# Even mixer of a four-layer model: values feature by feature, bias table and its products earlier, the first chunk's convolution taps on ScalarE and GpSimd

## The chip, the cores and the metric

The kernel runs on one core of a Trainium2 chip. The metric is the device time of one execution in microseconds (us), given as the median of several runs. The engines are called PE (TensorE, matrix products), DVE (VectorE), ACT (ScalarE), POOL (GpSimd) and SP (SyncE, which here issues DMAs). PE's clock has two levels, 1.2 and 2.4 GHz; the profile gives the granted clock of a stretch as a share of the higher one.

## The reference, cut to what matters

The model runs a row of blocks over 512 tokens of 1024 features. The change touches one mixer of them, attention beside a gated convolution, which runs once:

```python
def _attn_conv_mixer(h, w_in, sinks, conv_w, conv_b, ln_g, ln_b, w_out, rel_bias):
    u = h @ w_in
    ...
    q = u[..., :o1].reshape(bsz, seq, N_Q_HEADS, HEAD_DIM)      # 8 heads of 64
    k = u[..., o1:o2].reshape(bsz, seq, N_KV_HEADS, HEAD_DIM)   # 2 heads of 64
    v = u[..., o2:o3].reshape(bsz, seq, N_KV_HEADS, HEAD_DIM)
    attn = _swa_sink_attention(q, k, v, sinks, rel_bias)        # window 128, bias table by distance
    glu = u[..., o3:o4] * jax.nn.sigmoid(u[..., o4:])           # 512 channels
    ... _causal_depthwise_conv(glu, conv_w, conv_b) ...         # 31 taps a channel
    ... _layernorm over the 512 channels, silu; then [attn, conv] @ w_out
```

The input of the mixer is a normalized residual stream, and its output is added to it.

## The kernel before

**Layout and products.** Activations lie feature by feature: 128 partitions hold 128 features, and the free axis is the 512 tokens. Each product with weights is done in three passes of fp32r matmuls, high part by high part, low part by high part and high part by low part (lines 510, 511, 512). A job is one load of 128 x 2048 weights, `w_raw`. ACT rounds it to `w_hi` (`split_w`, line 1109), DVE takes the difference `w_lo` (line 1684), and then PE runs the job's two segments: each is one accumulation of 24 matmuls of 128x512 into one PSUM bank. `w_hi` and `w_lo` have two buffers, so ACT and DVE prepare the next job while PE works on this one.

**The even mixer's stages.** "ein" is six jobs, q = 0 to 5. Jobs 0 to 3 give the gated convolution's input: from each, DVE makes one chunk of 128 channels (two evictions, `hid` and `taps_in`, line 2230), ACT the sigmoid (line 1474), and DVE the product `glu` (line 2233). Jobs 4 and 5 give the queries `eq`. "einv" is one job whose first half gives the keys (`kz`) and whose second half the values (`vz`). Then follow eight attention units (two head groups of four tokens' blocks each), and "wout1", the output product.

**The convolution.** There are four chunks, c = 0 to 3, of 31 taps each. Chunk 3 has 21 of its taps on PE, as products with diagonal matrices (`taps`, line 960), `TAPS_EACH` of them in a unit. The last tap of chunks 0 to 2 is a seed that ACT writes to `cy` (line 1477). All 100 other taps are DVE instructions that read `cy`, add a shifted `glu` times a column of weights, and write `cy` (`conv_taps`, line 2217): eight after each "ein" job from q = 1 on, the others behind the key's evictions, between the four `eb_lo`, and in the units.

**The bias.** A small product of `onehot` and `relb` (line 884) makes a row of biases by distance. DVE adds the mask (`diag`), SP writes it to `diag_scratch` and reads it back as a table `ebias`. PE turns that table with four products by `flip` (line 907, "flips"), ACT and DVE keep a high and a low part of each (`eb_hi` line 1483, `eb_lo` line 2262). All four must be there before the first scores.

**The unit loop.** In each step u, PE has the scores of unit u (`qk`, lines 924 to 926), the transposes of unit u - 2 (`turn`, line 937) and the products with the values of unit u - 3 (`pv`, line 948). The scores go to DVE for maxima, to ACT for exponentials, to POOL for normalizing. Two units fill one bank with a pair of heads' output, which ACT and DVE split to `e_hi[r]`, `e_lo[r]` for r = 0 to 3 (`keep_o(r)`, line 2293); `pv` of the next pair waits until the bank has been read. At the steps `LN_AT = (6, 8)` PE sums over channels for the layer norm (`layer_sums`, line 974): `layer_sums(0)` gives the mean, which DVE subtracts, ACT squares, and `layer_sums(1)` the variance. Behind that come ACT's root (line 1535), DVE's reciprocal (line 2322) and four multiplications of `cy` (line 2326), ACT's four silu (line 1508) and `e_hi` (line 1541), DVE's four `e_lo` (line 2330), and "wout1".

**What sets the order.** Every engine's instruction stream is in the order in which the code writes it, and semaphores hold an instruction until its inputs are there. No scheduler moves anything. On PE, `pv(6, 0)` stands ahead of "wout1" and waits for `keep_o(2)`. On DVE, `keep_o(2)` is written into step u = 8, ahead of the four multiplications of `cy`.

Of the kernel before, what the change touches and what calls it, by code (L numbers as in the profile page):

```python
# [31 lines left out]
P = 128  # L32
T = 512
# [51 lines left out]
STAGES += [("up2", 22, 16, 2), ("down2", 16, 11, 1), ("ein", 6, 16, 2), ("einv", 1, 16, 5), ("wout1", 4, 16, 2),  # L85
# [20 lines left out]
for _name in PREPS:  # L106
    H_COUNT[_name] = _at
    if _name in GAIN:
# [4 lines left out]
             "ein": 12, "einv": 1, "rec": 4, "lgate": 0, "rec_b": 4, "ogate": 8}  # L113
# [37 lines left out]
CS_BANKS = (2, 3, 4, 7)  # L151
Q_BANKS = (0, 1, 6)
# [3 lines left out]
TAPS_AT, TAPS_EACH, LN_AT = 0, 5, (6, 8)  # L156
UNITS = 2 * NH
LAM_STEPS = 18
# [37 lines left out]
def build(nc, a, stop_after=None):  # L196
    with ExitStack() as ctx:
# [155 lines left out]
        kvc_done = sem("kvc_done")  # L353
# [21 lines left out]
        glu_sig, glu_done, y_seed, y_tap, y_made = (sem(n) for n in ("glu_sig", "glu_done", "y_seed", "y_tap", "y_made"))  # L375
        bias_hi, ident_kept, taps_made, zeroed = sem("bias_hi"), sem("ident_kept"), sem("taps_made"), sem("zeroed")
        k_kept, v_kept, sinks_neg = sem("k_kept"), sem("v_kept"), sem("sinks_neg")
# [129 lines left out]
        def _(pe):  # L507
# [370 lines left out]
            def even():  # L878
# [3 lines left out]

                pe.wait_ge(e_loaded, 16 * 5)
                pe.matmul(bank[MISC][0:8, 0:BLOCK_F + 1], relb[:], onehot[:], start=True, stop=True).then_inc(diag_mm, 1)

                j = J0["einv"]
                pe.wait_ge(w_lo_done, j + 1)
                pe.wait_ge(acc_free, FREE0["einv"] - 3)
                for k in range(ND):
                    mm = three(bank[0][:], *tile_of(j % 2, k), h_hi[:, k], h_lo[:, k], k == 0, k == ND - 1)  # L890
                mm.then_inc(seg_done, 1)
                for t in range(NT):
                    pe.wait_ge(acc_free, FREE0["einv"] + t - 2)
                    cols = slice(t * P, (t + 1) * P)
                    for k in range(ND):
                        wh, wl = tile_of(j % 2, ND + k)
                        mm = three(bank[(t + 1) % 4][:, 0:P], h_hi[:, k, cols], h_lo[:, k, cols], wh, wl, k == 0,
                                   k == ND - 1)
                    mm.then_inc(seg_done, 1)
                pe.wait_ge(diag_vec, 1)  # L900
                turn_rs(PREP_OF["mixe"] + 1)

                pe.wait_ge(diag_in, 16)
                for i in range(4):
                    if i >= 2:
                        pe.wait_ge(bias_kept, i - 1)
                    pe.matmul(bank[5 + i % 2][:], flip[:], ebias[:, 2 * i:2 * i + 2].rearrange("p h s -> p (h s)"),
                              start=True, stop=True).then_inc(flipped, 1)

                def qk(u, t):  # L910
# [4 lines left out]
                    if u == 0 and t == 0:  # L915
                        pe.wait_ge(bias_kept, 4)
                        pe.wait_ge(ident_kept, 1)
                        pe.wait_ge(k_kept, 2)
                        pe.wait_ge(v_kept, NT)
                        pe.wait_ge(zeroed, 2)  # L920
# [7 lines left out]
                def turn(u, x):  # L928
# [3 lines left out]
                    if u >= 1:  # L932
                        pe.wait_ge(kept_a, 2 * (u - 1) + x + 1)
                    for kb in (2 * x, 2 * x + 1):
                        for t in range(kb, min(kb + 2, NT)):
                            to, at = (kb % 2 * 2 + t - kb) * P, P if t == kb else 0
                            mm = pe.transpose(bank[4 + x][:, to:to + P], eprobs[u % 3][:, t, at:at + P], ident[:])
                    mm.then_inc(turned, 1)

                def pv(u, x):  # L940

                    r, half = u // 2, u % 2
                    if half == 0 and x == 0 and r:
                        pe.wait_ge(o_lo_done, ND + r)
# [7 lines left out]
                def taps(first, last):  # L952

                    for tap in range(first, min(last, PE_TAPS)):
                        if tap == 0:
# [3 lines left out]
                            pe.wait_ge(rs_col_done, 2)  # L959
# [18 lines left out]
                for u in range(E_UNITS + 3):  # L978
                    now, back, last = u < E_UNITS, 2 <= u < E_UNITS + 2, u >= 3
                    if now:  # L980
                        qk(u, 0)
                        qk(u, 1)
                    if back:
                        turn(u - 2, 0)
# [113 lines left out]
        def _(act):  # L1098
# [368 lines left out]
            def even():  # L1467
                for c in range(6):
# [6 lines left out]
                    if 1 <= c < 4:  # L1475
                        act.wait_ge(glu_done, c)
                        act.activation(cy[:, c - 1], glu[:, c - 1, TAPS - 1:], ACT.Identity, bias=col("cb_b", c - 1),
                                       scale=col("cb_w", (TAPS - 1) * CC + c - 1)).then_inc(y_seed, 1)
                act.activation(ident_r[:], ident[:], ACT.Copy).then_inc(ident_kept, 1)
                split_w(J0["wout1"])  # L1480
                for i in range(4):
                    act.wait_ge(flipped, i + 1)
                    act.activation(eb_hi[:, 2 * i:2 * i + 2].rearrange("p h s -> p (h s)"), bank[5 + i % 2][:], ACT.Copy,
                                   scale=1.0 / QK_SCALE).then_inc(bias_hi, 1)

# [191 lines left out]
        def _(dve):  # L1677
# [270 lines left out]
            def rope_end(r, out):  # L1948
# [12 lines left out]
                if r == 4:  # L1961
                    for half in range(2):
# [3 lines left out]
                        ins.then_inc(roped if half else kvc_done, 1)  # L1966
# [21 lines left out]
            def attention_inputs():  # L1988
# [9 lines left out]
                for q in range(4):  # L1998
                    for n in (2 * q, 2 * q + 1):
                        dve.wait_ge(seg_done, SEG0["kproj"] + n + 1)  # L2000
                        if n < 4:

                            for half in range(2):
                                src = slice(half * HD, (half + 1) * HD)
                                g = 2 * (n % 2) + half
                                dve.tensor_tensor(kvc[0:HD, n // 2, g * T:(g + 1) * T], bank[n % 4][src], rs[src], ALU.mult).then_inc(kvc_done, 1)
                                ins = dve.tensor_tensor(kvc[HD:P, n // 2, g * T:(g + 1) * T - 1], bank[n % 4][src, 1:T],
                                                        rs[src, 1:T], ALU.mult)
                                ins.then_inc(acc_free if half else kvc_done, 1)
# [190 lines left out]
            def even():  # L2200

                todo = [(0, tap) for tap in range(TAPS - 1)]
                todo += [(c, tap) for tap in range(TAPS - 1) for c in (1, 2)] + [(CC - 1, tap) for tap in range(PE_TAPS, TAPS)]
                place = {step: i for i, step in enumerate(todo)}
                tapped_now = 0

                def conv_taps(count, end=3 * (TAPS - 1)):
                    nonlocal tapped_now
                    count = min(count, end - tapped_now)
                    for c, tap in todo[tapped_now:tapped_now + count]:  # L2210
                        if (c, tap - 1) in place:
                            dve.wait_ge(y_tap, place[c, tap - 1] + 1)
                        else:
# [3 lines left out]
                        dve.scalar_tensor_tensor(out=cy[:, c], in0=glu[:, c, tap:tap + T], scalar=col("cb_w", tap * CC + c),  # L2217
                                                 in1=cy[:, c], op0=ALU.mult, op1=ALU.add).then_inc(y_tap, 1)
# [3 lines left out]
                for q in range(6):  # L2222
# [650 lines left out]
```

## Time and profile before

| | |
|---|---|
| median of 3 runs | 3060.1 us (3057.92 to 3061.3) |
| profiled execution, its own time | 3060.17 us |
| its span in the trace | 3058.4 us |
| PE busy | 2989.5 us, 98% |
| DVE, ACT, POOL busy | 52%, 39%, 17% |
| mean granted clock of PE | 0.991 |

The span runs from the first instruction of the trace to the last; 1.8 us of the execution's time lie outside it. The even mixer, with the start of its output product, covers 1592 to 1775 us of the span.

### The profile page before, as it was taken

The numbers are of one execution on the slowest core, as the hardware profiler recorded it, in microseconds if no ns is written. First come the engines' busy times: TensorE is split into PE (matmuls) and PEld (weight loads), VectorE is DVE, ScalarE is ACT, GpSimd is POOL, SyncE is SP. The second block draws the span as 40 slices with busy tenths as digits, with TensorE's granted clock in tenths as the row PEclk, the third lists the DMA queues.
The fourth block names the chain that finished last, engine by engine and source line by source line (L and its number), as shares of the span: only waits on it lengthen the run. The fifth ranks groups of instructions, "written<-read, shape, count | busy, mean of one in ns | idle before, by whom it ended". The sixth has DMA issues, their size and how long they took to land.

```text
span 3058.4 us, 37147 instructions
## 1 busy us (share of the span) xinstructions
PE 2989.5 (98%) x13546; PEld 2455.6 (80%) x13546; DVE 1594.9 (52%) x1838; ACT 1194.0 (39%) x1589; POOL 528.3 (17%) x516
## 2 busy tenths in 40 slices
PE   7999999999999999999999899999999999999998
PEld 6888877777888888788887688888888887788887
DVE  6665366687566535533338843333433337743332
ACT  5554243488455424322232442222322226532221
POOL 1111011255211112111110211111111104511110
PEclk9999999999999999999999999999999999999999
DMA  4222333200222223222232022222322232222222
GB/s 165 96 96 84 101 119 102 76 1 1 86 97 98 83 94 113 96 96 92 85 112 85 15 83 96 96 89 95 106 96 96 82 110 97 83 97 96 92 86 84
DMA packets 47931, 273.42 MB, mean 89 GB/s; under 512 B 6448, under 2 KB 8160, under 8 KB 25568
## 3 DMA queue, kind: packets, MB, share of 16 engines
q1 hardware_dynamic: 47840, 272.19, 25.7%
q8 instruction: 58, 0.95, 0.1%
q14 instruction: 33, 0.27, 0.0%
HBM read 269.28 MB, written 2.11 MB: 89 GB/s over the span
## 4 chain that ended last, share of the span: by engine, by line
PE 89%; DVE 6%; ACT 2%; issue 1%; POOL 1%; DMA 0%; DVEq 0%; ACTq 0%; SPq 0%; POOLq 0%
PE bank L510 28%; PE bank L512 28%; PE bank L511 28%; PE bank L822 1%; DVE w_lo L1684 1%; ACT probs L1394 1%; PE bank L960 1%; PE bank L728 0%; PE bank L806 0%; DVE rc L2395 0%; PE bank L839 0%; PE bank L838 0%; PE bank L926 0%; PE bank L807 0%; POOL r_lo L2674 0%
## 5 line engine op out<-in xcount | busy, mean ns | idle before, releaser
L510 PE MATMUL bank<-h_hi,w_hi 128*128 128x512 f32 x2448 | 961.7, 393 | 12.9 <-DVE w_lo L1684 7.8
L511 PE MATMUL bank<-h_lo,w_hi 128*128 128x512 f32 x2448 | 955.6, 390 | 0.0
L512 PE MATMUL bank<-h_hi,w_lo 128*128 128x512 f32 x2448 | 955.5, 390 | 0.0
L1684 DVE TENSOR_TENSOR w_lo<-w_raw,w_hi 128x2048 fp32r<-128x2048 f32 (+2 forms) x282 | 575.3, 2041 | 527.8 <-ACT w_hi L1109 527.1
L1109 ACT ACTIVATE w_hi<-w_raw 128x2048 fp32r<-128x2048 f32 (+2 forms) x282 | 474.9, 1684 | 328.3 <-PE bank L512 301.1
L510 PEld LDWEIGHTS bank<-h_hi,w_hi 128*128 128x128 f32 x2448 | 460.3, 188 | 117.0 <-DVE w_lo L1684 11.3
L512 PEld LDWEIGHTS bank<-h_hi,w_lo 128*128 128x128 f32 x2448 | 460.5, 188 | 97.3
L511 PEld LDWEIGHTS bank<-h_lo,w_hi 128*128 128x128 f32 x2448 | 460.5, 188 | 96.4 <-issue 1.9
L510 PE MATMUL bank<-act_hi,w_hi 128*128 128x512 f32 x1056 | 411.6, 390 | 4.4 <-DVE w_lo L1684 4.4
L511 PE MATMUL bank<-act_lo,w_hi 128*128 128x512 f32 x1056 | 411.3, 390 | 0.0
L512 PE MATMUL bank<-act_hi,w_lo 128*128 128x512 f32 x1056 | 411.3, 389 | 0.0
L2542 POOL TENSOR_TENSOR act_lo<-hid,act_hi 128x512 f32 (+1 forms) x132 | 171.8, 1301 | 1274.5 <-ACT act_hi L1202 847.3
L2517 POOL TENSOR_TENSOR sq_sum<-sq_sum,sq 128x512 f32<-128x512 f32 x87 | 123.5, 1420 | 824.3 <-ACT sq L1139 824.3
L510 PEld LDWEIGHTS bank<-act_hi,w_hi 128*128 128x128 f32 x1056 | 198.3, 188 | 46.3 <-DVE w_lo L1684 5.6
L1813 DVE TENSOR_TENSOR hid<-bank,rs 128x512 f32<-128x512 f32 x88 | 60.9, 692 | 331.6 <-PE bank L512 331.6
L512 PEld LDWEIGHTS bank<-act_hi,w_lo 128*128 128x128 f32 x1056 | 198.3, 188 | 41.3
L511 PEld LDWEIGHTS bank<-act_lo,w_hi 128*128 128x128 f32 x1056 | 198.3, 188 | 41.1
L1202 ACT ACTIVATE act_hi<-hid 128x512 f32 (+1 forms) x88 | 55.8, 634 | 410.8 <-DVE hid L1816 410.8
L1136 ACT ACTIVATE h_hi<-x,vec 128x512 fp32r<-128x512 f32 (+1 forms) x72 | 51.9, 723 | 366.2 <-DVE x L1701 366.2
L1701 DVE SCALAR_TENSOR_TENSOR x<-bank,x 128x512 f32 (+1 forms) x72 | 49.7, 691 | 254.1 <-PE bank L512 254.1
L1200 ACT ACTIVATE silu_g<-taps_in 128x512 f32<-128x512 f32 x88 | 55.7, 633 | 264.3 <-DVE taps_in L1810 264.3
L1786 DVE SCALAR_TENSOR_TENSOR bank<-taps_in,vec,bank 128x512 f32<-128x512 f32 x176 | 120.0, 750 | 1.8 <-ACT bank L1174 1.8
(373 smaller groups left out, 3207.3 us busy)
## 6 DMA issues: line engine op xcount, KB each, us to landing
w_raw<-in_w_up SPq DMA_DIRECT2D x132, 1024.0 KB, 4.9
w_raw<-in_w_down SPq DMA_DIRECT2D x96, 704.0 KB, 4.0
w_raw<-in_w_wout SPq DMA_DIRECT2D x12, 1024.0 KB, 4.9
w_raw<-in_w_ple SPq DMA_DIRECT2D x16, 640.0 KB, 3.9
w_raw<-in_w_ein SPq DMA_DIRECT2D x6, 1024.0 KB, 4.9
w_raw<-in_w_kproj SPq DMA_DIRECT2D x4, 1024.0 KB, 5.1
w_raw<-in_w_qproj SPq DMA_DIRECT2D x4, 1024.0 KB, 4.9
w_raw<-in_w_ogate SPq DMA_DIRECT2D x4, 1024.0 KB, 4.9
```

The lines of the kernel that those rows point to most:

```text
L510: pe.matmul(out, wh, mh, start=first, stop=False)
L511: pe.matmul(out, wh, ml, start=False, stop=False)
L512: return pe.matmul(out, wl, mh, start=False, stop=final)
L1109: act.activation(w_hi[j % 2][:, 0:n], w_raw[j % 2][:, 0:n], ACT.Copy).then_inc(w_hi_done, 1)
L1136: act.activation(h_hi[:, m], x[:, m], ACT.Copy, scale=col(GAIN[prep], m)).then_inc(h_hi_done, 1)
L1200: act.activation(silu_g[:], taps_in[:, u, PAD:], ACT.Silu).then_inc(silu_done, 1)
L1202: act.activation(act_hi[:, f], hid[:, u], ACT.Copy).then_inc(act_hi_done, 1)
L1684: dve.tensor_tensor(w_lo[j % 2][:, 0:n], w_raw[j % 2][:, 0:n], w_hi[j % 2][:, 0:n].bitcast(F32), ALU.subtract).then_inc(w_lo_done, 1)
L1786: dve.scalar_tensor_tensor(out=acc, in0=taps_in[:, g, PAD - back:PAD - back + T], scalar=col(f"conv{l}_{tap}", g * NF + f), in1=acc, op0=A ...
L1813: dve.tensor_tensor(hid[:, u], bank[2 * u + 1][:], rs[:], ALU.mult).then_inc(acc_free, 1)
L2517: pool.tensor_tensor(sq_sum[:], sq_sum[:], sq[:], ALU.add).then_inc(sq_added, 1)
L2542: pool.tensor_tensor(act_lo[:, f], hid[:, u], act_hi[:, f].bitcast(F32), ALU.subtract)\
```

## The change

**Values.** The value product becomes feature by feature like the keys: one segment of 24 matmuls of 128x512 into bank 4, where there were 96 matmuls of 128x128 with the tokens as the output's partitions. DVE scales it by the norm factor into `hid`, PE transposes it in four blocks (`turn_values`) between the first scores and the first taps, and ACT copies the result into `vz` with two instructions. DVE's eight small evictions and the transposes of the norm factor for them go.

**Bias.** The `onehot` product moves from behind q = 5 to behind q = 3, and DVE's `diag` to q = 4, so that the scratch's two DMAs are issued earlier. The four flips move between the key and the value product, into four banks of their own. On ACT the four `eb_hi` move ahead of `split_w` of "wout1".

**Taps.** Chunk 0's 30 taps leave DVE. ACT multiplies the shifted `glu` by the tap's column into `sq` or `silu_g` in turn, six such products in each "ein" step from c = 1 on (`first_products`), and POOL adds them to `cy` one after the other. Product t waits until the sum t - 2 is done, since it writes the tile that this sum read. Chunks 1 and 2 gather in PSUM banks 5 and 6, and move to `cy` in SBUF with the last tap before the units. DVE has 70 taps left, 31 in the "ein" steps, 6 behind the four `eb_lo`, 33 in the units. `TAPS_EACH` goes from 5 to 6, and `LN_AT` from (6, 8) to (5, 7). `keep_o(2)` is no longer pulled forward.

The settings and PE:

```diff
-TAPS_AT, TAPS_EACH, LN_AT = 0, 5, (6, 8)
+TAPS_AT, TAPS_EACH, LN_AT = 0, 6, (5, 7)
...
+FIRST_TAPS, EIN_TAPS = 8, {2: 8, 3: 8, 4: 8, 5: 7}
...
+                    if q == 3:
+                        pe.wait_ge(e_loaded, 16 * 5)
+                        pe.matmul(bank[MISC][0:8, 0:BLOCK_F + 1], relb[:], onehot[:], start=True, stop=True)\
+                            .then_inc(diag_mm, 1)
...
+                part_of(bank[0][:], 0)
+                pe.wait_ge(acc_free, FREE0["einv"])
                 pe.wait_ge(diag_vec, 1)
-                turn_rs(PREP_OF["mixe"] + 1)
-
                 pe.wait_ge(diag_in, 16)
                 for i in range(4):
-                    if i >= 2:
-                        pe.wait_ge(bias_kept, i - 1)
-                    pe.matmul(bank[5 + i % 2][:], flip[:], ebias[:, 2 * i:2 * i + 2].rearrange("p h s -> p (h s)"),
+                    pe.matmul(bank[FLIP_BANKS[i]][:], flip[:], ebias[:, 2 * i:2 * i + 2].rearrange("p h s -> p (h s)"),
                               start=True, stop=True).then_inc(flipped, 1)
+                part_of(bank[4][:], ND)
```

ACT:

```diff
+                def first_products(start, end):
+
+                    for tap in range(start, end):
...
+                        if tap >= 2:
+                            act.wait_ge(y_tap_first, tap - 1)
+                        act.activation(part_of_tap[tap % 2], glu[:, 0, tap:tap + T], ACT.Copy, scale=col("cb_w", tap * CC))\
+                            .then_inc(y_part, 1)
...
                 for c in range(6):
                     split_w(J0["ein"] + c + 1)
...
+                    if c >= 1:
+                        first_products(6 * (c - 1), 6 * c)
                 act.activation(ident_r[:], ident[:], ACT.Copy).then_inc(ident_kept, 1)
-                split_w(J0["wout1"])
```

DVE in the unit loop, and POOL:

```diff
-                    if u >= 5 and u % 2 == 1 and u != LN_AT[1] + 1:
+                    if u >= 5 and u % 2 == 1:
                         conv_taps(1, all_taps)
                         keep_o((u - 5) // 2)
...
                         dve.wait_ge(ln_vec, CC + 1)
-                        keep_o((u - 4) // 2)
                         for c in range(CC):
                             dve.tensor_tensor(cy[:, c], cy[:, c], rs[:], ALU.mult).then_inc(ln_vec, 1)
...
+                for tap in range(TAPS - 1):
+                    pool.wait_ge(y_part, tap + 1)
+                    if tap:
+                        pool.wait_ge(y_tap_first, tap)
+                    pool.tensor_tensor(cy[:, 0], cy[:, 0], part_of_tap[tap % 2], ALU.add).then_inc(y_tap_first, 1)
```

**Place 1: ACT, "ein" steps c = 1 and 2.** `w_hi` is the split of the next job's weights, `taps_in` a chunk's sigmoid, `cy` a seed. Before:

```order
L1109 ACTIVATE w_hi<-w_raw 128x2048
L1474 ACTIVATE taps_in<-taps_in 128x512
L1477 ACTIVATE cy<-glu,vec 128x512
L1109 ACTIVATE w_hi<-w_raw 128x2048
L1474 ACTIVATE taps_in<-taps_in 128x512
```

After:

```order
L1134 ACTIVATE w_hi<-w_raw 128x2048
L1511 ACTIVATE taps_in<-taps_in 128x512
L1515 ACTIVATE cy<-glu,vec 128x512
L1502 ACTIVATE sq<-glu,vec 128x512
L1502 ACTIVATE silu_g<-glu,vec 128x512
L1502 ACTIVATE sq<-glu,vec 128x512
L1502 ACTIVATE silu_g<-glu,vec 128x512
L1502 ACTIVATE sq<-glu,vec 128x512
L1502 ACTIVATE silu_g<-glu,vec 128x512
L1134 ACTIVATE w_hi<-w_raw 128x2048
L1511 ACTIVATE taps_in<-taps_in 128x512
```

Between a seed and the next `w_hi` there was nothing, and six products now stand there; the same six stand ahead of the `w_hi` of the jobs q = 3, 4, 5 and of "einv".

**Place 2: PE, from the key product to the first scores.** The rows of `h_hi` and `w_hi` are the weight products, `flip` the turned bias, `eb_hi` the first row of the scores. Before, the end of the value product and what follows:

```order
L510 MATMUL bank<-w_hi,h_hi 128x128
L511 MATMUL bank<-w_lo,h_hi 128x128
L512 MATMUL bank<-w_hi,h_lo 128x128
L639 MATMUL bank<-ident,rs 128x128 x4
L907 MATMUL bank<-ebias,flip 128x512 x4
L924 MATMUL bank<-eb_hi,ident_r 128x128
```

After, first the end of the key product and the start of the value product, then the end of that:

```order
L527 MATMUL bank<-h_hi,w_lo 128x512
L916 MATMUL bank<-ebias,flip 128x512 x4
L525 MATMUL bank<-h_hi,w_hi 128x512
L526 MATMUL bank<-h_lo,w_hi 128x512
L527 MATMUL bank<-h_hi,w_lo 128x512
```

```order
L525 MATMUL bank<-h_hi,w_hi 128x512
L526 MATMUL bank<-h_lo,w_hi 128x512
L527 MATMUL bank<-h_hi,w_lo 128x512
L940 MATMUL bank<-eb_hi,ident_r 128x128
L941 MATMUL bank<-eb_lo,ident_r 128x128
```

The flips stood directly ahead of the scores, and now a whole segment of 128x512 products stands between them.

**Place 3: DVE, the end of the unit loop.** `e_lo<-bank,e_hi` is `keep_o`, `rs` the layer norm's reciprocal, `cy<-cy,rs` its four multiplications, `e_lo<-cy,e_hi` the split of its result. Before:

```order
L2322 RECIPROCAL rs<-rs 128x512
L2293 TENSOR_TENSOR e_lo<-bank,e_hi 128x512
L2326 TENSOR_TENSOR cy<-cy,rs 128x512 x4
L2330 TENSOR_TENSOR e_lo<-cy,e_hi 128x512 x4
L2293 TENSOR_TENSOR e_lo<-bank,e_hi 128x512
L1684 TENSOR_TENSOR w_lo<-w_raw,w_hi 128x2048
```

After:

```order
L2329 RECIPROCAL estat<-estat 128x4
L2363 RECIPROCAL rs<-rs 128x512
L2366 TENSOR_TENSOR cy<-cy,rs 128x512 x4
L2370 TENSOR_TENSOR e_lo<-cy,e_hi 128x512 x4
L2334 TENSOR_TENSOR e_lo<-bank,e_hi 128x512 x2
L1730 TENSOR_TENSOR w_lo<-w_raw,w_hi 128x2048
```

`keep_o(2)` stood between the reciprocal and the multiplications, and now stands behind the last `e_lo` of the layer norm, with `keep_o(3)`. On ACT its `e_hi` moved in the same way, behind the four silu.

## Rows read from the trace of the kernel before

**Rows 1.** Windows: length, busy of PE, PEld, DVE, ACT, POOL, clock, DMA.

```profile
1592.00:1658.00 66.00, 66.00 (x289) 53.82 (x288) 51.62 (x57) 20.31 (x19) 8.66 (x4) 1.00 0.21 75
...
1740.00:1770.00 30.00, 24.40 (x95) 18.44 (x95) 14.07 (x18) 17.67 (x32) 2.25 (x5) 0.83 0.00 1
```

**Rows 2.** Chain that ended last: start, us, what; from q = 3 to the scores.

```profile
1625.92 0.38 PE bank L510
...
1658.92 0.74 PE bank L884 x2
...
1682.77 0.33 PE bank L924
```

**Rows 3.** ACT timeline, "ein": start, us, what, idle before and its releaser.

```profile
1617.05 1.91 ACT L1109 ACTIVATE w_hi<-w_raw 128x2048 fp32r<-128x2048 f32 x1
...
1639.19 1.91 ACT L1109 ACTIVATE w_hi<-w_raw 128x2048 fp32r<-128x2048 f32 x1
```

**Rows 4.** DVE timeline, "ein".

```profile
1623.46 2.28 DVE L1684 TENSOR_TENSOR w_lo<-w_raw,w_hi 128x2048 fp32r<-128x2048 f32 x1
...
1634.43 2.29 DVE L1684 TENSOR_TENSOR w_lo<-w_raw,w_hi 128x2048 fp32r<-128x2048 f32 x1
```

**Rows 5.** ACT timeline behind "wout1", 128x512 instructions.

```profile
1772.51 0.72 ACT L1136 ACTIVATE h_hi<-x,vec 128x512 fp32r<-128x512 f32 x1 [5.67 <-DVE x L1701]
1773.14 0.62 ACT L1139 ACTIVATE sq<-x 128x512 f32<-128x512 f32 x1
```

**Rows 6.** POOL timeline, sums elsewhere in the program.

```profile
33.64 1.28 POOL L2517 TENSOR_TENSOR sq_sum<-sq_sum,sq 128x512 f32<-128x512 f32 x1 [0.74 <-ACT sq L1139]
...
609.04 1.26 POOL L2578 TENSOR_TENSOR oq<-qr,oq 64x512 fp32r<-64x512 f32 x1 [0.17 <-POOL oq L2578]
...
2636.24 3.32 POOL L2674 TENSOR_TENSOR r_lo<-sq,r_hi 128x512 fp32r<-128x512 f32 x1
```

**Rows 7.** DVE timeline, one kind of instruction at two places.

```profile
34.15 1.32 DVE L1696 SCALAR_TENSOR_TENSOR h_lo<-x,vec,h_hi 128x512 fp32r<-128x512 f32 x1
...
1773.35 0.75 DVE L1696 SCALAR_TENSOR_TENSOR h_lo<-x,vec,h_hi 128x512 fp32r<-128x512 f32 x1 [0.87 <-ACT h_hi L1136]
```

**Rows 8.** PE timeline, first flips and the end of the unit loop.

```profile
1676.29 1.88 PE L907 MATMUL bank<-ebias,flip 128*128 128x512 f32 x4
...
1740.60 1.47 PE L948 MATMUL bank<-eturned,vz 128*128 128x256 f32 x4 [2.15 <-DVE e_lo L2293]
...
1745.53 0.60 PE L937 MATMUL bank<-ident,eprobs 128*128 128x128 f32 x4
...
1748.12 1.96 PE L974 MATMUL bank<-hid,ones 128*128 128x512 f32 x4
...
1756.69 2.07 PE L948 MATMUL bank<-eturned,vz 128*128 128x256 f32 x4 [4.45 <-DVE e_lo L2293]
...
1762.54 0.47 PE L510 MATMUL bank<-e_hi,w_hi 128*128 128x512 f32 x1
...
1765.33 0.50 PE L510 MATMUL bank<-e_hi,w_hi 128*128 128x512 f32 x1 [0.40 <-DVE e_lo L2330]
```

**Rows 9.** Chain that ended last, behind the second layer sums.

```profile
1751.83 0.70 ACT rs L1535
1752.55 3.37 DVE rs L2322
```

**Rows 10.** ACT timeline, silu and splits of the layer norm; squares before them.

```profile
1747.34 1.16 ACT L1532 ACTIVATE hid<-cy 128x512 f32<-128x512 f32 x2
...
1757.27 0.81 ACT L1508 ACTIVATE cy<-cy,vec 128x512 f32<-128x512 f32 x1 [2.47 <-DVE cy L2326]
...
1759.44 0.49 ACT L1504 ACTIVATE eturned<-bank 128x384 f32<-128x384 f32 x1 [1.36 <-PE bank L937]
1759.83 0.62 ACT L1541 ACTIVATE e_hi<-cy 128x512 fp32r<-128x512 f32 x1
...
1761.18 0.63 ACT L1541 ACTIVATE e_hi<-cy 128x512 fp32r<-128x512 f32 x1
```

More of the change, by code:

```diff
@@ L84 @@
     STAGES += [(f"up{_l}", 22, 16, 2), (f"down{_l}", 16, 11, 1), (f"ple{_l}", 8, 10, 2)]
-STAGES += [("up2", 22, 16, 2), ("down2", 16, 11, 1), ("ein", 6, 16, 2), ("einv", 1, 16, 5), ("wout1", 4, 16, 2),
+STAGES += [("up2", 22, 16, 2), ("down2", 16, 11, 1), ("ein", 6, 16, 2), ("einv", 1, 16, 2), ("wout1", 4, 16, 2),
            ("up3", 22, 16, 2), ("down3", 16, 11, 1), ("up4", 22, 16, 2), ("down4", 16, 11, 1),
@@ L155 @@
 PE_TAPS = 21
-TAPS_AT, TAPS_EACH, LN_AT = 0, 5, (6, 8)
+TAPS_AT, TAPS_EACH, LN_AT = 0, 6, (5, 7)
 UNITS = 2 * NH
+FIRST_TAPS, EIN_TAPS = 8, {2: 8, 3: 8, 4: 8, 5: 7}
+TAP_STEPS = [(1, _t) for _t in range(FIRST_TAPS)]
+for _t in range(TAPS - 1 - FIRST_TAPS):
+    TAP_STEPS += [(1, FIRST_TAPS + _t), (2, _t)]
+TAP_STEPS += [(2, _t) for _t in range(TAPS - 1 - FIRST_TAPS, TAPS - 1)]
+TAP_STEPS += [(CC - 1, _t) for _t in range(PE_TAPS, TAPS)]
+TAP_PLACE = {_s: _i for _i, _s in enumerate(TAP_STEPS)}
+IN_BANK = sum(EIN_TAPS.values()) + 6
+MOVED_AT = {_c: 1 + max(_i for _i, _s in enumerate(TAP_STEPS[:IN_BANK]) if _s[0] == _c) for _c in (1, 2)}
 LAM_STEPS = 18
@@ L881, in even, with part_of @@
                           after=lambda n: stats("mixe") if n == 0 else None)
-                pe.wait_ge(e_loaded, 16 * 5)
-                pe.matmul(bank[MISC][0:8, 0:BLOCK_F + 1], relb[:], onehot[:], start=True, stop=True).then_inc(diag_mm, 1)
+                    if q == 3:
+                        pe.wait_ge(e_loaded, 16 * 5)
+                        pe.matmul(bank[MISC][0:8, 0:BLOCK_F + 1], relb[:], onehot[:], start=True, stop=True)\
+                            .then_inc(diag_mm, 1)
                 j = J0["einv"]
+                def part_of(out, at):
+                    for k in range(ND):
+                        mm = three(out, *tile_of(j % 2, at + k), h_hi[:, k], h_lo[:, k], k == 0, k == ND - 1)
+                    mm.then_inc(seg_done, 1)
@@ L908, in even, with turn_values @@
                               start=True, stop=True).then_inc(flipped, 1)
+                part_of(bank[4][:], ND)
+                def turn_values():
+                    pe.wait_ge(acc_free, FREE0["einv"] + 2)
+                    for t in range(NT):
+                        cols = slice(t * P, (t + 1) * P)
+                        mm = pe.transpose(bank[4][:, cols], hid[:, 0, cols], ident[:])
+                    mm.then_inc(v_turned, 1)
                 def qk(u, t):
@@ L1476, in even @@
                         act.wait_ge(glu_done, c)
[L1477 removed]
+                        to = cy[:, 0] if c == 1 else bank[ACC_BANKS[c - 1]][:]
+                        act.activation(to, glu[:, c - 1, TAPS - 1:], ACT.Identity, bias=col("cb_b", c - 1),
                                        scale=col("cb_w", (TAPS - 1) * CC + c - 1)).then_inc(y_seed, 1)
+                    if c >= 1:
+                        first_products(6 * (c - 1), 6 * c)
                 act.activation(ident_r[:], ident[:], ACT.Copy).then_inc(ident_kept, 1)
[L1480 removed]
                 for i in range(4):
                     act.wait_ge(flipped, i + 1)
[L1483 removed]
+                    act.activation(eb_hi[:, 2 * i:2 * i + 2].rearrange("p h s -> p (h s)"), bank[FLIP_BANKS[i]][:], ACT.Copy,
                                    scale=1.0 / QK_SCALE).then_inc(bias_hi, 1)
+                split_w(J0["wout1"])
+                act.wait_ge(zeroed, 2)
+                act.wait_ge(v_turned, 1)
+                for half in range(2):
+                    cols = slice(half * HD, (half + 1) * HD)
+                    act.activation(vz[:, half, :, cols], bank[4][:].rearrange("p (t q) -> p t q", t=NT)[:, :, cols], ACT.Copy)\
+                        .then_inc(v_kept, 1)
                 def exps(u):
```

113 lines of the change are left out of this document (57 added, 56 removed).

## The prediction

> **What bounds the kernel now.** I read the windows of the mixer first, then the chain that ended last, then the timelines of the engines that PE waits for. In the windows PE is busy for all of the 66.0 us of "ein" at a granted clock of 1.00, and for 24.4 of the 30 us of the tail at 0.83 [rows 1]. So "ein" has nothing to win on PE, but every wait put there costs; the tail already waits. The first row also gives a price: 289 matmuls in 66.0 us, 0.228 us each, so 5.45 us for a segment of 24 and 10.9 us for a job. The chain shows where PE is released by others: between the key product (1658.92 + 0.74 = 1659.66) and the first scores at 1682.77 the value product ends and DVE's evictions and bias splits follow, with PE waiting [rows 2]. In "ein", ACT's `w_hi` of job q = 3 had ended at 1617.05 + 1.91 = 1618.96 [rows 3], yet DVE began that job's `w_lo` only at 1623.46 [rows 4], behind its taps, and PE started the job at 1625.8 [rows 2]: 2.34 us from the start of a `w_lo` to the first matmul, with no slack left.
>
> **Part A: six products ahead of each `w_hi`.** Chunk 0's taps leave DVE, and six products now stand on ACT between a seed and the next job's `w_hi`. Free of the sums, a product is nearest to ACT's 128x512 instruction with a column scale: 0.72 us long, 0.63 from start to start [rows 5]. Six would take 3.9 us. They are not free: product t waits for sum t - 2, so in a group the sixth waits for the fourth sum. A sum of two 128x512 tiles takes POOL 1.28 us, and a sum that waits for the one before starts 0.17 us behind it [rows 6]: 1.45 from one to the next. A group then lasts 0.72 + 4 x 1.45 + 0.63 = 7.2 us.
>
> For q = 3 the `w_hi` moves from 1617.05 to 1624.25, so it ends at 1626.2; add 0.3 for the last sums beside `w_lo` (below) and 2.34, and PE starts at 1628.8 instead of 1625.8: +3.0. For the next jobs I need the loop without products: from the start of a `w_lo` (1634.43) over the evictions, the sigmoid, `glu` and the seed to the next `w_hi` (1639.19) is 4.76, and its 1.91 follows: 6.67 [rows 3, 4]. With 7.2 and 0.3 it is 14.2 us a job against PE's 10.9: +3.3 at q = 4 and at q = 5. Together 9.6. The split for "einv" has no sigmoid ahead and is in time. The bias row of 0.74 moves into one of these waits: -0.7. PE's clock: in the tail the waits go with a granted 0.83 [rows 1], so the matmuls behind a wait are slow; behind the first two it only fills the next wait, behind the last it counts. In the tail 24.4 busy us at 0.83 lose 4.1, behind three waits (at 1740.60, 1756.69 and 1765.33 [rows 8]): 1.4 for one, which I take, between 0 and 4.1. 9.6 - 0.7 + 1.4: **A = +10.3.** Bounds: 6 with sums 1.3 us apart, no lock and no slow clock; 13.5 if each `w_lo` also waits out most of a sum (1.28). Behind the waiting products ACT has only `w_hi` and the next sigmoid; behind the sums POOL has the normalizing of the units, which comes later than all of this.
>
> The lock: beside a POOL sum of 1.28 us, DVE's splitting instruction with two SBUF inputs took 1.32 us, and 0.75 far from any sum [rows 6, 7]; so DVE waits up to 0.6 there. `w_lo` starts about 2.5 us behind the group's fourth sum while two more need 2.9, whence 0.3. The other way round, a sum that stood beside a DVE `w_lo` took 3.32 [rows 6].
>
> The Trainium skill ("SBUF — State Buffer", section "Who interferes with whom") has it that a DVE instruction with two SBUF inputs and a GpSimd instruction that reads SBUF exclude each other for a whole instruction, and that a DVE instruction with at most one SBUF input does not contend. The rows above agree with the first half. By the rule the taps of chunks 1 and 2, whose accumulator is now in PSUM, leave the sums alone, which speaks against the second rival; without the rule's lock A would be 0.9 lower, 9.4.
>
> **Part B: bias and values.** Before, 1659.66 to 1682.77 is 23.1 us [rows 2]. Now PE has the key segment, four flips and the value segment: 5.45 + 4 x 0.86 + 5.45 = 14.3, with 0.86 for a flip from 1.88 for two [rows 8], whose last 0.17 overlaps what follows. The bias splits on ACT and DVE, which PE waited for, now lie under the value segment: behind the last flip there are one `eb_hi` and one `eb_lo`, some 1.4 us by the 0.72 and 0.75 of such instructions [rows 5, 7], against 5.45. Without that cover they would cost those 1.4. The scratch's DMAs go out before the key product instead of in it, and "wout1"'s loads, behind them on SP's queue, go earlier too; nothing waits for them. The two `vz` copies, the scaled values and the 31 + 6 DVE taps stand beside the units. The four transposes take the place of those of the norm factor. **B = -8.8.**
>
> **Part C: the unit loop up to the second layer sums.** Six taps a unit instead of five only shift PE's 21. `layer_sums(1)` comes a step earlier, so one turn and `pv`, from 1745.53 to 1748.12, fall behind it: -2.6 [rows 8]. Against that, the work that hid DVE's and ACT's chain behind the first sums is one step shorter: `pv(4, 0)` already waited 2.15 us for `keep_o` [rows 8], and its `e_hi(1)` now stands behind the four squares (1.16 for two, so 2.2 [rows 10]) and a unit's exponentials. Bounds: -2.6 if that wait doesn't grow, +4 if both delays add in full and the clock falls once more. I take **C = +1.3**, nearer the upper end, because in the row the wait is there already.
>
> **Part D: from the second layer sums to "wout1".** Before, 1751.83 to 1762.54, 10.7 us; and the nine matmuls up to 1765.33 took 2.8 where 9 x 0.228 = 2.05, for the layer norm's `e_lo` came late: 0.7 more [rows 8, 9]. 11.4. Now `pv(6, 0)`, which stands ahead of "wout1" on PE, waits for `keep_o(2)`, and that stands behind the whole layer norm on both engines. The root 0.72 and the reciprocal 3.4 [rows 9]; a multiplication to the first silu 0.7 (the reciprocal ended at 1755.92 and the first silu came at 1757.27 with the old `keep_o`, about 0.65, between them); four silu with their `e_hi` 1.35 apart, 5.4; two copies of turned probabilities at 0.4 (1759.44 to 1759.83); `e_hi(2)` 0.6 and `e_lo(2)` 0.7 [rows 10]: 0.7 + 3.4 + 0.7 + 5.4 + 0.8 + 1.3 = 12.3. Then the last products of the units, 1756.69 to 1762.54, 5.85 at the low clock [rows 8]; I take 5.0 (bounds 4.4 and 5.85), for part of the turns are now done ahead. 17.3 less 11.4: **D = +5.9** (5.3 to 6.8). Behind the waiting `pv` stands all of "wout1", whose layer norm half would be ready.
>
> **Sum.** 10.3 - 8.8 + 1.3 + 5.9 = +8.7. The profiled execution took 3060.17 us (span 3058.4 and 1.8 around it), the median is 3060.1, so the sum holds for either: **3068.9 us**. All lower bounds together give -0.1 (6.0 - 8.8 - 2.6 + 5.3), all upper ones +15.5 (13.5 - 8.8 + 4 + 6.8); its own range is 3064 to 3074. A measurement of this kernel can tell about 0.2%, 6.1 us, from no change.
>
> **The rivals.** *First, the products don't hold `w_hi` up* (the other side, not slower). Place: ACT in q = 2 to 5. For q = 3 `w_hi` may be 4.5 us later than 1617.05 (1623.46 less 1618.96) before PE waits, and six bare products need 3.9. So it decides at sums of about 0.7 us. Then A is 0 and the time 3060.2 - 8.8 + 1.3 + 5.9 = 3058.6. Against it: no sum of this size is near that, 1.28 being the undisturbed one [rows 6]. 0.10. *Second, the sums are slower than 1.28*, since `glu`, `w_lo` and DVE get in between. At 1.7 us a group is 1.7 us longer and three jobs add 5: 3074; at 2.0, with the "einv" job late as well, 3.6 more: 3077 to 3083. For it: 3.32 beside a `w_lo`; against: in most of a group DVE has no instruction with two SBUF inputs. 0.15. *Third, loop and tail cancel*: C is -2.6, and D only +3 since `pv` and turns that move behind the sums fill part of the wait: 3060.2 + 10.3 - 8.8 - 2.6 + 3 = 3062. 0.13. The forecast keeps 0.60, with 0.08 of it below 3066.3. First and third together would give 3052, 0.02.
>
> **How the numbers follow.** Slower by over 0.2%: 0.52 of the forecast, 0.15, 0.04 of the third: 0.71. Faster: 0.05 (both mild rivals together, and the low end of the first). Same: 0.24. The range takes in the third rival and the lower half of the second; what is left out is most of the first and of the second's high end: 3060 to 3077.
>
> **What would show it.** Right: PE idle some 3 us ahead of jobs q = 3, 4 and 5, put down to `w_lo`; ACT's `w_hi` about 7 us behind the seed; POOL's sums 1.45 apart; the first scores about 14.5 us behind the key product's start; `pv(6, 0)` starting some 12 us behind the second layer sums. Wrong: sums closer than 0.8 or wider than 1.7; no wait ahead of q = 4; `pv(6, 0)` in less than 8 us; the flips waiting for the table.

## The result and the profile after

The changed kernel takes 3067.45 us (median of 14 runs, 3063.99 to 3069.38) where the kernel before takes 3060.18 (14 runs): a ratio of 1.0025, with a 95% interval of 1.0018 to 1.0031. It is slower by 7.3 us, forecast were 8.7, inside the range of 3060 to 3077. The profiled execution took 3069.19 us (span 3067.4), near the slow end of its runs, while that of before lay at its median; so the traces differ by 9.0, not 7.3.

The page puts more waiting for `w_lo` ahead of the first pass (line 525 now), where before it was 7.8 of 12.9 us:

```profile
L525 PE MATMUL bank<-h_hi,w_hi 128*128 128x512 f32 x2456 | 965.7, 393 | 18.6 <-DVE w_lo L1730 13.4
```

The windows of "ein" and of the tail (columns as in [rows 1]):

```profile
1617.00:1631.00 14.00, 11.32 (x44) 8.92 (x44) 4.42 (x5) 7.30 (x10) 7.75 (x6) 0.90 0.12 36
...
1645.00:1659.00 14.00, 11.30 (x44) 8.94 (x43) 10.41 (x14) 7.99 (x11) 12.22 (x9) 0.88 0.10 43
1659.00:1671.00 12.00, 12.00 (x54) 9.91 (x54) 10.26 (x14) 6.72 (x9) 10.78 (x8) 1.00 0.80 262
```

"Ein", which kept PE busy throughout [rows 1], now has two holes of 2.7 us, ahead of q = 3 and q = 5, and the granted clock of those windows is 0.90 and 0.88. ACT's timeline from the first seed to the next `w_hi`:

```profile
1616.02 0.80 ACT L1515 ACTIVATE cy<-glu,vec 128x512 f32<-128x512 f32 x1
1616.73 0.71 ACT L1502 ACTIVATE sq<-glu,vec 128x512 f32<-128x512 f32 x1
1617.34 0.71 ACT L1502 ACTIVATE silu_g<-glu,vec 128x512 f32<-128x512 f32 x1
1618.93 0.72 ACT L1502 ACTIVATE sq<-glu,vec 128x512 f32<-128x512 f32 x1 [0.88 <-POOL cy L2666]
1620.36 0.73 ACT L1502 ACTIVATE silu_g<-glu,vec 128x512 f32<-128x512 f32 x1 [0.71 <-POOL cy L2666]
...
1623.24 0.72 ACT L1502 ACTIVATE silu_g<-glu,vec 128x512 f32<-128x512 f32 x1 [0.71 <-POOL cy L2666]
1623.88 1.90 ACT L1134 ACTIVATE w_hi<-w_raw 128x2048 fp32r<-128x2048 f32 x1
```

Two products go at once, and each further one waits for a sum. POOL's sums at the start of that group and, further on, beside a `w_lo`; then DVE's `w_lo` for q = 3:

```profile
1617.61 1.29 POOL L2666 TENSOR_TENSOR cy<-cy,sq 128x512 f32<-128x512 f32 x1 [14.79 <-ACT sq L1502]
1619.04 1.29 POOL L2666 TENSOR_TENSOR cy<-cy,silu_g 128x512 f32<-128x512 f32 x1
...
1654.23 2.90 POOL L2666 TENSOR_TENSOR cy<-cy,sq 128x512 f32<-128x512 f32 x1 [0.39 <-ACT sq L1502]
```

```profile
1625.81 2.42 DVE L1730 TENSOR_TENSOR w_lo<-w_raw,w_hi 128x2048 fp32r<-128x2048 f32 x1 [8.96 <-ACT w_hi L1134]
```

PE's timeline, from q = 3 to the first scores (the four flips are the eight matmul records of line 916), and the end of the unit loop with "wout1":

```profile
1628.28 0.79 PE L525 MATMUL bank<-h_hi,w_hi 128*128 128x512 f32 x1 [2.68 <-DVE w_lo L1730]
...
1640.99 0.81 PE L899 MATMUL bank<-onehot,relb 32*8 32x384 f32 x2
...
1642.18 0.50 PE L525 MATMUL bank<-h_hi,w_hi 128*128 128x512 f32 x1 [0.38 <-DVE w_lo L1730]
...
1656.05 0.79 PE L525 MATMUL bank<-h_hi,w_hi 128*128 128x512 f32 x1 [2.70 <-DVE w_lo L1730]
...
1673.88 3.60 PE L916 MATMUL bank<-ebias,flip 128*128 128x512 f32 x8
1682.77 0.22 PE L940 MATMUL bank<-eb_hi,ident_r 128*128 128x128 f32 x1
...
1745.09 2.07 PE L971 MATMUL bank<-eturned,vz 128*128 128x256 f32 x4 [3.50 <-DVE e_lo L2334]
...
1753.88 1.02 PE L997 MATMUL bank<-silu_g,ones 128*128 128x512 f32 x2
...
1767.34 2.07 PE L971 MATMUL bank<-eturned,vz 128*128 128x256 f32 x4 [9.71 <-DVE e_lo L2334]
...
1772.82 0.47 PE L525 MATMUL bank<-e_hi,w_hi 128*128 128x512 f32 x1
```

Ahead of q = 4 PE waits only 0.38 us. Behind the first hole, the 48 matmuls of q = 3 take 12.7 us (1628.28 to the bias row at 1640.99) where they took 11.1 before, so the slower clock fills most of the next wait.

The wait ahead of `pv(6, 0)` is 9.7 us, where it was 4.45 [rows 8]. The chain that ended last shows what fills it, from the root to the late `keep_o(2)`:

```profile
1754.94 0.69 ACT rs L1581
1755.66 3.37 DVE rs L2363
...
1766.07 0.49 ACT e_hi L1563
1766.59 0.70 DVE e_lo L2334
1767.34 2.07 PE bank L971 x4
```

To add this up I take from each trace the times from the first matmul of "ein" (1592.22 before, 1591.90 after): to the flips, to the first scores, then from there to the end of the second layer sums, and on to the first matmul of the next stage. The table has them for all kernels of this study; one profiled execution each, in us. The last column is PE's granted clock from the scores to the second sums.

| kernel | to flips | to scores | scores to second sums | on to next stage | in all | clock |
|---|---|---|---|---|---|---|
| before | 84.1 | 90.6 | 69.0 | 55.1 | 214.7 | 0.95 |
| after | 82.0 | 90.9 | 72.1 | 61.6 | 224.6 | 0.93 |
| keep_o(2) early | 82.2 | 91.0 | 70.1 | 53.6 | 214.8 | 0.95 |
| old LN_AT | 81.9 | 90.8 | 69.3 | 55.2 | 215.3 | 0.98 |
| five tiles | 73.4 | 82.3 | 72.0 | 61.5 | 215.8 | 0.93 |
| products behind `w_hi` | 72.7 | 81.8 | 74.4 | 61.6 | 217.8 | 0.95 |
| values and bias alone | 72.8 | 81.6 | 72.2 | 55.2 | 209.0 | 0.98 |
| accumulators in SBUF | 92.2 | 101.1 | 71.6 | 62.5 | 235.1 | 0.95 |
| five tiles, old LN_AT | 73.5 | 82.4 | 70.7 | 55.2 | 208.2 | 0.95 |
| five tiles, keep_o(2) early | 73.5 | 82.4 | 72.1 | 54.3 | 208.8 | 0.91 |

Since the flips were behind the value product before, their column compares only the kernels that have them in the new place. The key product begins 5.45 us ahead of the flips now, so at 76.5 us, where it was at 1659.66 - 1592.22 = 67.4: part A is +9.1. To the scores it is +0.3 in all, so B is -8.8; then C is +3.1 in this execution and D +6.4. The sum is 9.8; other stages take back 0.8.

### The profile page after: what moved, and what is told of

The parts are those of the page before. It is cut to its first block, busy times and chain, and to the rows that moved or that the text cites. A ratio compares the mean times of both kernels' runs of the same rounds, so it can differ in the third digit from the quotient of the medians.

```text
span 3067.4 us, 37059 instructions
## 1 busy us (share of the span) xinstructions
PE 2986.8 (97%) x13474; PEld 2451.4 (80%) x13474; DVE 1573.8 (51%) x1800; ACT 1215.1 (40%) x1621; POOL 568.9 (19%) x546
## 4 chain that ended last, share of the span: by engine, by line
PE 88%; DVE 7%; ACT 3%; issue 1%; POOL 1%; DMA 0%; DVEq 0%; ACTq 0%; SPq 0%; POOLq 0%
PE bank L525 27%; PE bank L526 27%; PE bank L527 27%; DVE w_lo L1730 1%; PE bank L837 1%; ACT probs L1419 1%; PE bank L982 1%; POOL cy L2666 1%; PE bank L743 0%; PE bank L821 0%; DVE rc L2435 0%; ACT w_hi L1134 0%; PE bank L971 0%; PE bank L853 0%; PE bank L854 0%
## 5 line engine op out<-in xcount | busy, mean ns | idle before, releaser
L525 PE MATMUL bank<-h_hi,w_hi 128*128 128x512 f32 x2456 | 965.7, 393 | 18.6 <-DVE w_lo L1730 13.4
```

The source lines that it names most:

```text
L525: pe.matmul(out, wh, mh, start=first, stop=False)
```

## The experiments

**1. keep_o(2) pulled forward again.** In the changed kernel, with `LN_AT` left at (5, 7). ACT's copies of unit 7's turned probabilities go ahead too, or they would wait behind the silu in its place.

The first line added is DVE's, in the step of the reciprocal; the others are ACT's, one step later.

```diff
                         dve.wait_ge(ln_vec, CC + 1)
+                        keep_o((u - 3) // 2)
                         for c in range(CC):
...
+                    if u >= 5 and u % 2 == 1 and u != LN_AT[1] + 2 or u == LN_AT[1] + 1:
+                        r = (u - 4) // 2 if u == LN_AT[1] + 1 else (u - 5) // 2
                         act.wait_ge(pv_done, 4 * (r + 1))
...
+                        keep(u - 1, 0)
                         silu_of(0)
+                        silu_of(1)
+                        keep(u - 1, 1)
```

> Theory (order of the queues in the tail): with keep_o(2) ahead of the layer norm's multiplications on DVE, and its e_hi and the copies of unit 7's turned probabilities ahead of the silu on ACT, pv(6, 0) starts some 5 us behind the second layer sums instead of 12.4, and "wout1" starts about 6.5 us earlier: 3061 us. Rival (the layer norm's own chain holds "wout1"): pv comes early, but "wout1" waits for the last e_lo and the time stays within 1.5 us of the changed kernel, 3066 to 3069 us.

Measured: 3059.97 us (11 runs), ratio to before 1.0001 [0.9992, 1.0010]. PE's timeline, the second layer sums' last row and `pv(6, 0)`:

```profile
1750.91 1.02 PE L997 MATMUL bank<-silu_g,ones 128*128 128x512 f32 x2
...
1756.82 1.13 PE L971 MATMUL bank<-eturned,vz 128*128 128x256 f32 x4 [2.17 <-DVE e_lo L2337]
```

`pv(6, 0)` starts 4.9 us behind the sums instead of 12.4, and the stretch to the next stage falls from 61.6 to 53.6. That is the theory; the layer norm alone does not hold "wout1". The column before it, 70.1 against 72.1, is not the edit's: up to there the two kernels do the same. The windows from `pv(2, 0)` to the first layer sums, of the changed kernel and of this one, show what differs:

```profile
1726.20:1731.10 4.90, 4.89 (x19) 4.22 (x20) 1.70 (x4) 0.56 (x2) 0.97 (x2) 0.65 0.00 0
```

```profile
1725.20:1728.50 3.30, 3.25 (x19) 2.95 (x20) 1.73 (x4) 0.42 (x2) 1.00 (x2) 1.00 0.00 0
```

The same matmuls, behind a wait of 2.75 and 2.74 us, run at a granted clock of 0.65, so for the most part at 1.2 GHz, in the one execution, and at 2.4 GHz in the other. That is 1.6 us of the 2.0. So a difference of 2 us in this column says little without the clock beside it.

**2. LN_AT, TAPS_EACH and keep_o as before.**

```diff
-TAPS_AT, TAPS_EACH, LN_AT = 0, 6, (5, 7)
+TAPS_AT, TAPS_EACH, LN_AT = 0, 5, (6, 8)
...
+                        keep_o((u - 4) // 2)
```

> The changed kernel with LN_AT (6, 8), TAPS_EACH 5 and keep_o pulled forward as before. Theory (parts C and D are losses of 3.1 and 6.5 us from this one choice): 3058 to 3060 us. Rival (the loop's loss comes from the values' new way into vz or from taps on DVE that now stand in the units): D goes, C stays, 3061 to 3063 us.

Measured: 3059.83 us (11 runs), ratio 1.0000 [0.9991, 1.0009]. PE's waits for `keep_o` ahead of `pv(2, 0)` and `pv(4, 0)`:

```profile
1724.50 1.13 PE L971 MATMUL bank<-eturned,vz 128*128 128x256 f32 x4 [2.00 <-DVE e_lo L2334]
...
1740.49 1.98 PE L971 MATMUL bank<-eturned,vz 128*128 128x256 f32 x4 [2.15 <-DVE e_lo L2334]
```

Both are as before (2.01 and 2.15), and the last stretch falls to 55.2, within 0.1 of before. So D, and the part of C that lies in these waits, come from the three settings that the edit puts back together. The stretch up to the second sums falls to 69.3, within 0.3 of before, but at a granted clock of 0.98 against 0.95; with the same code in the units experiment 7 has 70.7 at 0.95. So up to 1.7 us there can come from elsewhere, the values' new way for one, and the traces don't settle it. What is left of the change is A and B, which cancel.

**3. Five tiles for the products.** A group of six then hardly waits for its own sums. The three further tiles are `cy`'s chunks 1 to 3, unused so far at that point; DVE waits for the last sum before it writes them.

```diff
-        y_part, part_of_tap = sem("y_part"), (sq[:], silu_g[:])
+        y_part, part_of_tap = sem("y_part"), (sq[:], silu_g[:], cy[:, 1], cy[:, 2], cy[:, 3])
...
-                        if tap >= 2:
-                            act.wait_ge(y_tap_first, tap - 1)
+                        if tap >= 5:
+                            act.wait_ge(y_tap_first, tap - 4)
...
```

> The products go to five tiles in turn instead of two, so a group of six hardly waits for sums. Theory (products wait for the sums): a group falls from 7.2 to about 4 us, the waits ahead of jobs q = 3, 4 and 5 fall from 9.1 us together to 0 to 2.5, and the time to 3060 to 3062 us. Rival (ACT's time in thirty products, or w_lo shut out by the sums that now run beside it): the waits keep at least two thirds of their 9.1 us and the time stays above 3064 us.

Measured: 3060.15 us (11 runs), ratio 1.0000 [0.9991, 1.0009]. ACT's timeline for the group that took 7.15 us above:

```profile
1616.78 0.71 ACT L1502 ACTIVATE sq<-glu,vec 128x512 f32<-128x512 f32 x1
1617.39 0.71 ACT L1502 ACTIVATE silu_g<-glu,vec 128x512 f32<-128x512 f32 x1
1618.01 1.94 ACT L1502 ACTIVATE cy<-glu,vec 128x512 f32<-128x512 f32 x3
1619.85 0.71 ACT L1502 ACTIVATE sq<-glu,vec 128x512 f32<-128x512 f32 x1
1620.46 1.90 ACT L1134 ACTIVATE w_hi<-w_raw 128x2048 fp32r<-128x2048 f32 x1
```

The same six products now take 3.7 us, and the flips come 8.6 us earlier. The only wait for `w_lo` left in "ein" is ahead of q = 4, where a `w_lo` beside the sums took 3.18 us:

```profile
1637.90 0.50 PE L525 MATMUL bank<-h_hi,w_hi 128*128 128x512 f32 x1 [0.54 <-DVE w_lo L1730]
```

It is not ACT's time in the products that cost, but their waiting for POOL, with `w_hi` behind them in the queue.

**4. Products behind the next `w_hi`.** Two tiles as in the change, only the order on ACT is other.

```diff
                     split_w(J0["ein"] + c + 1)
...
+                    if c >= 2:
+                        first_products(6 * (c - 2), 6 * (c - 1))
...
-                    if c >= 1:
-                        first_products(6 * (c - 1), 6 * c)
+                first_products(24, 30)
```

> Each group of six products moves behind the next job's w_hi, two tiles as in the change. Theory (what costs in "ein" is only that w_hi stands behind the group): no wait for w_lo ahead of jobs q = 3 and 5 and under 1.5 us ahead of q = 4; but the last group now ends later than the flips, and the first scores and the transposes of the values wait, so of the 9 us some 3 to 6 come back: 3062 to 3065 us. Rival (POOL's sums or w_lo beside them set "ein"): the waits in "ein" stay above 5 us together and the time above 3066 us.

Measured: 3064.93 us (10 runs), ratio 1.0017 [1.0008, 1.0026]. All waits for `w_lo` ahead of q = 3, 4 and 5 are gone (72.7 us to the flips), but the transposes of the values wait on PE:

```profile
1677.75 0.66 PE L925 MATMUL bank<-ident,hid 128*128 128x128 f32 x4 [3.16 <-DVE hid L2307]
```

The last group on ACT now ends at 1669.9, so the bias splits come late; the scores hardly notice, but DVE's six taps stand behind the splits and the scaled values behind those taps. The units pay 2.3 us by the table (74.4 against 72.1), or 4.3 against experiment 1's execution at the same clock of 0.95. The median lies 3.0 us above the profiled execution (3061.89), so its trace shows less of the loss than the medians do. Two experiments with opposite means, free tiles and another order, so take the same 9 us out of "ein".

**5. Accumulators of chunks 1 and 2 in SBUF.** The changed kernel with the taps' accumulators in `cy`, as before, so that a tap has two SBUF inputs.

```diff
-                        to = cy[:, 0] if c == 1 else bank[ACC_BANKS[c - 1]][:]
+                        to = cy[:, c - 1]
...
-                        held = c in ACC_BANKS and i < MOVED_AT[c]
+                        held = False
```

> The changed kernel with the accumulators of chunks 1 and 2 in SBUF, as before, so that DVE's taps have two SBUF inputs while the sums run. Theory (sums and such taps exclude each other): a sum beside taps rises from 1.43 to above 2 us from start to start, a tap from 0.7 to above 1, the groups ahead of jobs q = 4 and 5 get some 4 us longer each, and the time is 3074 to 3090 us. Rival (the place of the accumulator does not matter to the sums): 3066 to 3070 us.

Measured: 3081.61 us (4 runs), ratio 1.0074 [1.0059, 1.0090], in the range of the theory. POOL's sums and DVE's taps of the same stretch:

```profile
1632.53 1.56 POOL L2666 TENSOR_TENSOR cy<-cy,silu_g 128x512 f32<-128x512 f32 x1
1634.23 1.56 POOL L2666 TENSOR_TENSOR cy<-cy,sq 128x512 f32<-128x512 f32 x1
```

```profile
1630.50 11.73 DVE L2266 SCALAR_TENSOR_TENSOR cy<-glu,vec,cy 128x512 f32<-128x512 f32 x8
1642.15 2.28 DVE L1730 TENSOR_TENSOR w_lo<-w_raw,w_hi 128x2048 fp32r<-128x2048 f32 x1
```

Eight taps with the accumulator in PSUM, in the same place of the changed kernel; then eight taps of the kernel before, in SBUF but with no sums beside them:

```profile
1630.88 6.30 DVE L2266 SCALAR_TENSOR_TENSOR bank<-glu,vec,bank 128x512 f32<-128x512 f32 x8
```

```profile
1628.25 6.26 DVE L2217 SCALAR_TENSOR_TENSOR cy<-glu,vec,cy 128x512 f32<-128x512 f32 x8
```

So neither the place nor the sums alone slow the taps; both together take them from 6.3 to 11.7 us. The sums are 1.70 us apart instead of 1.43, less than I expected (above 2). So the cost of q = 4 and 5 went another way than I had it: `w_lo` stood behind slow taps on DVE. Further on the groups on ACT did get longer, for there the taps held up a sum:

```profile
1663.10 6.89 POOL L2666 TENSOR_TENSOR cy<-cy,sq 128x512 f32<-128x512 f32 x1
```

```profile
1663.46 5.37 DVE L2266 SCALAR_TENSOR_TENSOR cy<-glu,vec,cy 128x512 f32<-128x512 f32 x8
```

**6. Values and bias alone.** The changed kernel with all taps on DVE in SBUF, no products, no sums, and `LN_AT`, `TAPS_EACH` and `keep_o` as before. DVE has three taps ahead of the four `eb_lo` and six behind them.

```diff
+EIN_TAPS = {q: 8 for q in range(1, 6)}
+TAP_STEPS = [(0, _t) for _t in range(TAPS - 1)]
+TAP_STEPS += [(_c, _t) for _t in range(TAPS - 1) for _c in (1, 2)]
+TAP_STEPS += [(CC - 1, _t) for _t in range(PE_TAPS, TAPS)]
...
-                    if c >= 1:
-                        first_products(6 * (c - 1), 6 * c)
...
+                conv_taps(3)
```

> Only the values and the bias are changed; taps, LN_AT, TAPS_EACH and keep_o as before. Theory (part B is a gain of 8.8 us that the other parts used up): 14.3 us from the key product to the first scores instead of 23.1, and 3051 to 3053 us, faster than both kernels. Rival (the gain is given back in the units, where DVE has as many taps as before but less time ahead of the units): the first scores come 8.8 us earlier, but the layer sums don't, and the time is 3056 us or more.

Measured: 3051.39 us (7 runs), ratio 0.9973 [0.9962, 0.9984]. The first scores come 8.9 us earlier, and the medians differ by 8.0. The rival is right to a third in the profiled execution: the units take 72.2 us instead of 69.0, with a wait of 1.27 us for the scaled values, whose eviction stands behind DVE's taps:

```profile
1675.51 0.66 PE L921 MATMUL bank<-ident,hid 128*128 128x128 f32 x4 [1.27 <-DVE hid L2283]
```

**7 and 8. The three losses taken out together.** Five tiles with the old `LN_AT`, and five tiles with `LN_AT` (5, 7) and `keep_o(2)` early: the edits of experiments 3 and 2, and of 3 and 1.

> Values, bias, five tiles for the products, and LN_AT, TAPS_EACH and keep_o as before the change. Theory (the three losses are independent): from the start of "ein" 82.3 us to the first scores as with five tiles, 69.3 to the second layer sums and 55.2 to the next stage as with the old LN_AT: some 2 us less than the values and bias alone, 3049 to 3051 us. Rival (with the wait in "ein" gone the units catch up with DVE's taps, and the loop loses again): 3052 us or more.

> Values, bias, five tiles, LN_AT (5, 7), and keep_o(2) pulled forward as in the first experiment. Theory: 82.3 us to the first scores, 70 to 72 to the second layer sums, 53.6 to the next stage: 3049 to 3052 us. Rival as for the run beside it: 3053 us or more.

Measured: 3051.06 us (7 runs), ratio 0.9971 [0.9959, 0.9982], and 3051.49 us (8 runs), ratio 0.9973 [0.9962, 0.9983]. In the first, the units take 70.7 us where 69.3 were expected, and the other two stretches are as expected (82.4 and 55.2). The 2 us ahead of the values and bias alone are not there in the medians: 3051.06 against 3051.39 can't be told apart. All three are some 8 us faster than the kernel before on the same chip, and the one with the fewest edits is as good as the others. Taking chunk 0's taps off DVE is worth nothing measurable here even where it costs nothing.

## Why the prediction was right, and where it was off

The forecast was made of four terms, and each has its experiment.

- **A**, forecast +10.3, measured +9.1. The group is as worked out: 7.15 us from the first product to `w_hi` (7.2 forecast), sums 1.43 to 1.45 apart. The jobs q = 3, 4 and 5 start 2.8, 5.7 and 8.6 us late where I had 3.0, 6.3 and 9.6. Two sizes were too large: the share of the lock, for `w_lo` took 2.42 to 2.45 us beside the last sums instead of 2.28, so 0.15, not 0.3; and the later groups, which took 7.05 us, not 7.2. For the clock behind the last wait I took 1.4, and q = 5's 48 matmuls took 12.4 us where a job at the full clock takes 10.9, so 1.5. (The start of q = 3 before, 1625.80 in PE's timeline, is 1625.92 in the row that the prediction names for it; that changes nothing here.) One sign did not come as I wrote it: PE is not idle for 3 us ahead of q = 4, but for 0.38, because the slow matmuls of q = 3 fill that wait, as the sum had it. The mechanism is shown twice, by experiments 3 and 4.
- **B**, forecast and measured -8.8; from the flips to the scores PE waits for nothing. Experiment 6 gives it by itself, at 3051.4 us, 8.0 less than before.
- **C**, forecast +1.3, measured +3.1 in the profiled execution, at a granted clock of 0.93, and +1.1 in that of experiment 1, which does the same up to there, at 0.95, the clock of the kernel before. So the size of this term is not settled to better than 2 us. Its mechanism I had only in part: I counted one wait that grows, ahead of `pv(4, 0)`, and it did (3.50 instead of 2.15). But two earlier ones grew as well, that of unit 5's scores and that of `pv(2, 0)`; before, then now:

```profile
1720.83 0.33 PE L924 MATMUL bank<-eb_hi,ident_r 128*128 128x128 f32 x1 [0.51 <-ACT eprobs L1494]
...
1724.66 1.13 PE L948 MATMUL bank<-eturned,vz 128*128 128x256 f32 x4 [2.01 <-DVE e_lo L2293]
```

```profile
1721.64 0.33 PE L940 MATMUL bank<-eb_hi,ident_r 128*128 128x128 f32 x1 [2.11 <-ACT eprobs L1540]
...
1726.21 1.13 PE L971 MATMUL bank<-eturned,vz 128*128 128x256 f32 x4 [2.75 <-DVE e_lo L2334]
```

The three grow by 3.7 us together, which less the 2.6 for the turn and `pv` that moved behind comes to the 1.1 of experiment 1. The +1.3 had 3.9 for one wait alone, so that it came near is luck. The growth goes with `LN_AT` and `TAPS_EACH`: in experiment 2, which puts both back, the three waits are 0.29, 2.00 and 2.15. With six taps a unit PE's 21 are used up one unit earlier, so unit 5's scores may wait longer for that reason alone; the two settings were not tried apart.

- **D**, forecast +5.9, measured 6.4. `pv(6, 0)` starts 12.4 us behind the sums (12.3 forecast), and the last products take 5.5 instead of 5.0. Experiment 1 removes it.

The sum came near the measured 7.3 in part because errors cancel: with C at +1.1 the four terms come to 7.8, and the 0.8 that other stages take back were not in the forecast.

The first rival, a free chain of sums, did not come, but experiment 3 shows its condition: with the products at 3.7 us the wait ahead of q = 3 is gone, as the slack of 4.5 us had it. The second, slower sums, stayed out because the accumulators are in PSUM: experiment 5, which takes that away, comes to 3081.6. The third, loop and tail cancelling, needed C at -2.6 and D at +3, and neither came.

On the second the Trainium skill ("SBUF — State Buffer", sections "SBUF: two separate sides" and "Who interferes with whom") speaks of exclusion for a whole instruction between a DVE instruction with two SBUF inputs and a GpSimd instruction that reads SBUF. The runs agree that such taps contend and taps with a PSUM accumulator don't, and in experiment 5 a sum was held for 6.89 us while eight taps ran at 0.67 each. But in its other groups a sum of 1.29 and a tap of 0.67 in strict turns would be 1.96 us apart, and the sums were 1.70 apart, so there a part of them overlaps.

## What to carry to other kernels

- An engine's free time is not enough to move work there. ACT was idle for some 8 us ahead of the sigmoids of chunks 1 to 3, and the products, which fit into it, were put in front of the one instruction of its queue that PE was waiting for, and chained to a third engine.
- A change of several parts is worth taking apart even when its total is small: 8.8 us of gain and, in the profiled execution, 18.6 of loss stood behind it, and the loss was in the parts that took taps off DVE, which here did not set the time of "ein", and that moved the layer norm forward.
- When the place of one stage in a loop is moved, look at what was pulled forward by hand around the old place; `keep_o(2)` cost 6 us by standing where the general rule put it.

## What was not expected of the hardware

Behind equal waits of 2.7 us PE's clock fell in one execution and not in another (experiment 1), and that alone moves the unit loop by 1.6 us: one profiled execution can't settle a term of that size. And contention for SBUF between DVE and POOL was not a matter of a small lock: with 128x512 taps it raised a tap from 0.79 to 1.47 us or stretched a sum from 1.29 to 6.89, and cost some 10 us between the profiled executions and 14 between the medians, or 15 with each taken against the kernel before on its own chip (experiment 5).
